# First raw pieces of the down product ahead of the last stores, the output weights split in the SSD's end, the mLSTM block's last iterations reordered

## The reference

```
x = x + (silu(h @ w_ffn_gate) * (h @ w_ffn_up)) @ w_ffn_down        # first block, last step
...
y_ssd = ssd_mixer(...)            # second block; scan over 8 chunks of 128 tokens
y_ml  = mlstm_mixer(...)          # the same chunks, 8 heads of 128
x  = x + concatenate([y_ssd, y_ml]) @ w_out
h2 = rmsnorm_2(x, norm2_w)
x  = x + hier_moe(h2, router_g_w, ..., exp_w_gate, exp_w_up, exp_w_down)
# hier_moe: best of 4 groups, then the best 2 of its 8 experts, for each token
```

## Time and the profile before

| quantity | value |
|---|---|
| median of 3 runs | 3291.56 us (3291.55 to 3295.12) |
| the profiled execution, its own time | 3288.88 us |
| its span in the profile | 3287.0 us |
| mean granted TensorE clock | 0.963 of full speed |
| PE busy | 3031.3 us, 92% of the span |
| PEld busy | 2485.2 us, 76% |
| DVE busy | 2204.8 us, 67% |
| ACT busy | 1617.9 us, 49% |
| POOL busy | 679.5 us, 21% |

### The profile page before, as it was taken

One profiled execution on the slowest core, in us unless ns is written; L12 is line 12 of the kernel. 1 busy time (PEld: TensorE's weight loads), 2 busy tenths in 40 slices (PEclk: granted clock), 3 DMA queues, 4 the chain that ended last, 5 costly groups with the idle time before them and its releaser, 6 DMA issues. The chain is left out here.

```text
span 3287.0 us, 38738 instructions
## 1 busy us (share of the span) xinstructions
PE 3031.3 (92%) x13814; PEld 2485.2 (76%) x13814; DVE 2204.8 (67%) x2760; ACT 1617.9 (49%) x2341; POOL 679.5 (21%) x553
## 2 busy tenths in 40 slices
PE   6999999899999999999899999979868779999994
PEld 4777777687878888788678886767767668888883
DVE  6668677624344545489477775449666579999997
ACT  6554444411343333345445443344354358888883
POOL 4222222100132222000322221134132111111100
PEclk9999999999999999999899999989989879999997
DMA  3222222442322223577254333352153079999995
GB/s 91 71 85 78 85 85 84 155 134 83 128 66 95 77 77 97 192 266 253 86 122 122 110 103 106 108 198 97 65 185 131 33 295 390 394 386 380 377 376 225
DMA packets 386898, 533.40 MB, mean 162 GB/s; under 512 B 68240, under 2 KB 268944, under 8 KB 385712
## 3 DMA queue, kind: packets, MB, share of 16 engines
q1 hardware_dynamic: 368064, 480.80, 42.4%
q0 software_dynamic: 18672, 50.49, 4.1%
HBM read 458.71 MB, written 89.26 MB: 167 GB/s over the span
## 5 line engine op out<-in xcount | busy, mean ns | idle before, releaser
L3883 DVE TENSOR_TENSOR h_hl<-ex_stage,h_hl 128x1024 fp32r<-128x1024 f32 x256 | 304.7, 1219 | 36.4 <-ACT h_hl L3879 34.7
L3879 ACT ACTIVATE h_hl<-ex_stage 128x1024 fp32r<-128x1024 f32 x256 | 271.2, 1061 | 74.3 <-PE ex_ps_d L430 24.3
L428 PE MATMUL m_ps<-m_t,m_ring 128*128 128x512 f32 x432 | 173.0, 400 | 13.4 <-DVE m_sga L842 5.0
L429 PE MATMUL m_ps<-m_t,m_ring 128*128 128x512 f32 x432 | 169.2, 392 | 0.0
L430 PE MATMUL m_ps<-m_t,m_ring 128*128 128x512 f32 x432 | 169.2, 392 | 0.0
L3883 DVE TENSOR_TENSOR ex_w_hl<-ex_stage,ex_w_hl 128x1024 fp32r<-128x1024 f32 x128 | 155.1, 1232 | 9.7 <-ACT ex_w_hl L3879 9.3
L687 ACT ACTIVATE m_ring<-m_sums 128x512 fp32r<-128x512 f32 x108 | 67.7, 628 | 166.7 <-POOL m_sums L663 115.6
L3879 ACT ACTIVATE ex_w_hl<-ex_stage 128x1024 fp32r<-128x1024 f32 x128 | 134.9, 1055 | 25.3 <-DMA ex_stage<-in_exp_w_gate_dram 12.6
L1603 DVE TENSOR_TENSOR ff_ring<-ff_stage,ff_ring 128x512 fp32r<-128x512 f32 x63 | 60.1, 953 | 110.1 <-ACT ff_ring L1517 109.4
L428 PE MATMUL ff_ps<-ff_t_high,ff_ring 128*128 128x512 f32 x336 | 130.8, 389 | 0.9 <-DVE ff_up_odd L1622 0.9
L430 PE MATMUL ff_ps<-ff_t_high,ff_ring 128*128 128x512 f32 x336 | 130.7, 389 | 0.0
(11 more groups left out here) (673 smaller groups left out, 9275.4 us busy)
## 6 DMA issues: line engine op xcount, KB each, us to landing
ex_stage<-in_exp_w_gate_dram SPq DMA_DIRECT2D x128, 512.0 KB, 5.4
ex_stage<-in_exp_w_up_dram SPq DMA_DIRECT2D x128, 512.0 KB, 5.4
ex_stage<-in_exp_w_down_dram SPq DMA_DIRECT2D x128, 512.0 KB, 5.4
m_stage<-in_w_in_dram SPq DMA_DIRECT2D x56, 512.0 KB, 4.7
ff_act_raw<-scratch_act SPq DMA_DIRECT2D x77, 256.0 KB, 3.4
ff_down_raw<-in_w_ffn_down_dram SPq DMA_DIRECT2D x77, 256.0 KB, 4.3
pc_stage<-in_w_in_dram SPq DMA_DIRECT2D x36, 512.0 KB, 5.1
ff_stage<-in_w_ffn_gate_dram SPq DMA_DIRECT2D x22, 512.0 KB, 3.7
```

What stands on the lines that cost most here:

```text
L428: nc.tensor.matmul(out, w_hl[0], x_hl[0], start=first, stop=False, skip_group_check=further)
L429: nc.tensor.matmul(out, w_hl[0], x_hl[1], start=False, stop=False, skip_group_check=further)
L3879: nc.scalar.activation(w_hl[u][:, 0], stage[:, s], ACT.Copy).then_inc(s_hi, 1)
L3883: nc.vector.tensor_tensor(w_hl[u][:, 1], stage[:, slot(e, u)], f32(w_hl[u][:, 0]), ALU.subtract).then_inc(s_lo, 1)
```

## The change

It has three parts. **In the feed-forward**, the raw buffers and slots are laid out anew, so that the third and fourth raw buffers are free when product 7 of the last block is done. SP issues the loads of steps 0 and 1 before the last store but one, those of steps 2 and 3 before the last store. `down_high(2)`, `down_low(1)` and `down_low(2)` move ahead of the last block's end. **In the SSD's end**, rows 0 to 6 of the mLSTM half of `w_out` are loaded in three DMAs (2, 2 and 3 rows of 128x1024) over the place of their low parts, and split there by seven ACT copies and seven DVE subtractions; in the mLSTM only the last row is left (two loads, two ACT copies, two POOL subtractions). `rows_g` is now requested ahead of queries and keys, and `chunk_loads(2)` and the gain row follow two weight loads instead of sixteen. **In the mLSTM's last iterations** the order on PE, DVE and ACT is written out; `choose` is cut into `group`, `best` and `second`, with additions and norms between them; the last chunk's split `y` has a buffer of its own, so that it waits for no output product; ACT's squares of tiles 6 and 7 use another scratch tile.

```diff
@@ hidden_memory
-    slot_at = [t_at(0, 0), t_at(1, 0), t_at(0, 1), t_at(0, 2), t_at(1, 2), t_at(0, 3), t_at(1, 3)]
+    slot_at = [t_at(0, 0), t_at(1, 0), t_at(0, 1), t_at(0, 3), t_at(1, 3), ring_at, ring_at + t_bytes]
...
-    raw_a = [room_at, t_at(1, 1), room_at + 2 * piece, ring_at]
-    raw_b = [room_at + piece, t_at(1, 1) + piece, ring_at + piece, ring_at + 2 * piece]
+    raw_a = [room_at, t_at(1, 1), room_at + 2 * piece, t_at(0, 2) + piece]
+    raw_b = [room_at + piece, t_at(1, 1) + piece, t_at(0, 2), t_at(1, 2)]
@@ feed_forward
-                product_done(eng, at[NF - 1, (5, 5, 6, 7, 7, 4, 4)[e]])
+                product_done(eng, at[NF - 1, (5, 5, 6, 4, 4, 3, 3)[e]])
...
                 elif e == 2:
-                    product_done(sp, N - 1)
+                    product_done(sp, at[NF - 1, 7])
...
-            for q in range(NF - 3, NF - 1):
-                store(q)
+            store(NF - 3)
             load(0)
             load(1)
+            store(NF - 2)
+            load(2)
+            load(3)
             store(NF - 1)
-            load(2)
-            for e in range(3, NE):
+            for e in range(4, NE):
...
+                elif seq[n - NR] == (NF - 1, 4):
+                    down_high(2)
             silu(NF - 1, 1, s_c12, NF - 1)
...
                     down_low(0)
+                    down_low(1)
                 elif seq[n - NR] == (NF - 1, 4):
-                    down_low(1)
+                    down_low(2)
             odd_act(NF - 1)
@@ ssd_chunks
+        FETCHED = (2, 4, NK)
+        w1_raw = Over(nc, at_hl + 8 * W * 4, at_hl + 16 * W * 4).take("w1_raw", [P, NK, W])
...
+            sp.wait_ge(p_state, NC)
+            sp.wait_ge(d_y, NC)
+            for sem, lo, hi in zip(s_w1, (0,) + FETCHED, FETCHED):
+                sp.dma_start(w1_raw[:, lo:hi], w1_v[:, lo:hi]).then_inc(sem, 16)
...
+            def w1_high(n):
+                act.wait_ge(s_w1[sum(n >= hi for hi in FETCHED)], 16)
+                nc.scalar.activation(hl[:, 0, n], w1_raw[:, n], ACT.Copy).then_inc(s_w1hi, 1)
...
+            def w1_low(n):
+                dve.wait_ge(s_w1hi, n + 1)
+                v.tensor_tensor(hl[:, 1, n], w1_raw[:, n], f32(hl[:, 0, n]), ALU.subtract)
...
+                if k == NC - 1:
+                    add(k - 1, (0,))
+                    w1_low(0)
+                    add(k - 1, (1,))
...
+            for n in range(1, NK):
+                w1_low(n)
             add(NC - 1)
@@ mlstm_chunks, SP
+                wait(sp, g_w, k - 2)
+                sp.dma_start(rows_g[:, b].rearrange("p h n -> p (h n)"), every(scr.rows[k, 0])).then_inc(s_rows[b], 16)
                 sp.dma_start(queries(k), scr.qk[k][:, 0:H]).then_inc(s_qk[b], 16)
                 sp.dma_start(keys(k), scr.qk[k][:, H:]).then_inc(s_qk[b], 16)
-                wait(sp, g_w, k - 2)
...
-            for n in range(NW):
-                h, k = divmod(n, KT)
-                low_ready(sp, n - NS)
-                sp.dma_start(stage[n % NS], w_v[:, k, h * HALF:(h + 1) * HALF]).then_inc(s_w[n % NS], 16)
-                if n == NW - 1:
-                    chunk_loads(2)
-                if n == NW - 1:
-                    sp.dma_start(gain_b[:], A.norm2_w_2[0].rearrange("(a n) -> a n", a=1).broadcast_to([P, W])).then_inc(s_gr, 16)
+            for h in range(2):
+                sp.dma_start(last_row_of[h], w_v[:, KT - 1, h * HALF:(h + 1) * HALF]).then_inc(s_w[h], 16)
+            chunk_loads(2)
+            sp.dma_start(gain_b[:], A.norm2_w_2[0].rearrange("(a n) -> a n", a=1).broadcast_to([P, W])).then_inc(s_gr, 16)
@@ mlstm_chunks, DVE, after the last chunk's query
+            gated(NC - 1)
+            y_low(NC - 1)
+            logits(NC - 4)
+            routing_tables()
+            group()
+            add(NC - 2, 1)
+            gained(NC - 3)
+            inverted(NC - 2)
+            normed_low(NC - 3)
+            best()
+            add(NC - 1, 0)
+            gained(NC - 2)
+            logits(NC - 3)
+            normed_low(NC - 2)
+            second()
+            early_totals()
+            add(NC - 1, 1)
+            logits(NC - 2)
+            inverted(NC - 1)
+            early_ranks()
+            gained(NC - 1)
...
+            early_slots(range(4))
+            normed_low(NC - 1)
+            early_slots(range(4, 2 * r.EARLY))
+            logits(NC - 1)
@@ mlstm_chunks, PE, last iteration and after it
+                if k == NC - 1:
+                    y_turn(k)
                 if 0 <= k - 3:
                     logit(k - 3)
...
+            out_product(NC - 1, 0)
+            normed_turn(NC - 2)
+            logit(NC - 3)
+            out_product(NC - 1, 1)
+            logit(NC - 2)
...
+            normed_turn(NC - 1)
+            logit(NC - 1)
```

More of the change, by code:

```diff
@@ L2609, in first_chunk, with ssd_chunks @@
     return head
-def ssd_chunks(nc, A, x_tm, at_hl, w2, scr, done, head, o_stored):
+def ssd_chunks(nc, A, x_tm, at_hl, w2, hl, scr, done, head, o_stored):
     NC, H, G, W = scr.T, SSD_HEADS, SSD_GROUPS, 1024
@@ L2774, in _ @@
                     decay(k + 1, 1)
+                else:
+                    for n in range(2):
+                        w1_high(n)
                 act.wait_ge(d_yt, 2 * k + 2)
@@ L2780, in _ @@
                 if k == NC - 1:
+                    for n in range(2, NK):
+                        w1_high(n)
                     act.wait_ge(head.g_w, 1)
@@ L3239, in _ @@
                 if k == 0:
-                    for n in range(6):
-                        w_high(n)
-                if t == 0:
-                    lows_ready(act, NW)
-                if t >= 0:
-                    act.wait_ge(d_add, 2 * t + 2)
-                    wait(act, n_lo, t)
-                    nc.scalar.activation(xg[:].rearrange("p k n -> p (k n)"), x_tm[:, t], ACT.Square,
-                                         accum_out=ssq[:, t:t + 1]).then_inc(n_sq, 1)
+                    w_high(0)
+                    w_high(1)
+                if 0 <= t < NC - 2:
+                    squares(t)
                 if k < NC:
@@ L3251, in _ @@
                     nc.scalar.activation(sm[:, STD], sm[:, VAR], ACT.Sqrt, scale=1.0 / D, bias=eps[:]).then_inc(a_std, 1)
-                if t >= 0:
-                    act.wait_ge(n_sq, t + 1)
-                    nc.scalar.activation(std[:, t:t + 1], ssq[:, t:t + 1], ACT.Sqrt, scale=1.0 / W, bias=eps[:]).then_inc(n_std, 1)
+                if 0 <= t < NC - 2:
+                    deviation(t)
                 if k < NC:
@@ L3269, in _ @@
                     nc.scalar.activation(r_hl[:, :, 0], r_st[:], ACT.Copy).then_inc(s_rhi, 1)
[L3270 to L3283 removed]
+                if 0 <= t < NC - 1:
+                    if t < NC - 2:
+                        scaled(t)
+                    if k == NC - 1:
+                        y_high(k)
+                        squares(t + 1)
+                        deviation(t + 1)
+                    normed_high(t)
+                    if k == NC - 1:
+                        scaled(t + 1)
+                if k < NC - 1:
+                    y_high(k)
+            squares(NC - 1)
+            deviation(NC - 1)
+            scaled(NC - 1)
+            normed_high(NC - 1)
         @block.vector
@@ L3569, in _, with normed_turn, y_turn @@
             pe.wait_ge(d_cs, 1)
-            for k in range(NC + 3):
-                if k < NC:
-                    numerators(k)
-                    updates(k, 0)
-                    updates(k, 1)
+            def normed_turn(t):
+                pe.wait_ge(n_xn, t + 1)
+                turn("x", t, lambda h: xn[:, h * P:(h + 1) * P])
+            def y_turn(k):
+                pe.wait_ge(a_hn, NJ * (k + 1))
+                turn("y", k, lambda h: h_r[:, h])
+            for k in range(NC):
+                numerators(k)
+                updates(k, 0)
+                updates(k, 1)
@@ L3600, in route @@
+            mm(ps_rank, r.before[:], r.early_o, start=True, stop=False)
+            mm(ps_rank, r.ones[:], r.early_counts[:, 0:r.EARLY], start=False, stop=True).then_inc(r_ranked, 1)
+            normed_turn(NC - 1)
+            logit(NC - 1)
 def route(nc, A, hl, scr, c, block, mem, r):
@@ L4332, in program @@
             done = [s for s in USED if s is not o_stored[0] and not any(s is k for k in head.sems)]
-            ssd_chunks(nc, A, x_tm, at_hl, w2_hl, scr, done, head, o_stored)
+            ssd_chunks(nc, A, x_tm, at_hl, w2_hl, hl, scr, done, head, o_stored)
             done = [s for s in USED if not any(s is k for k in head.sems)]
```

266 lines of the change are left out of this document (128 added, 138 removed).

## The result

| | before | with the change |
|---|---|---|
| median | 3291.56 us (4 runs) | 3264.89 us (3263.34 to 3268.53, 4 runs) |
| ratio to before | 1 | 0.9926, 95% interval 0.9913 to 0.9938 |
| profiled execution, own time | 3288.88 us | 3268.53 us |
| its span | 3287.0 us | 3266.7 us |

The change makes the kernel 26.7 us faster by the medians, 24.4 by the ratio. The number on record was 3261.5 (-30), so the direction and the size hold. The profiled execution is the slowest of its four, and stages that the change doesn't touch differ by some 2 us between two traces. So stages are compared here by their own lengths, from an event at their start to one at their end.

What follows compares the result with a forecast made beforehand. PE, busy for 92% of the span, bounds the kernel, so gains come only where it stands still: -5 + 0 - 13 - 12 = -30 from 3288.88, 3258.9; 3261.5 us for the median, range 3255 to 3275.

Steps and rivals of the forecast that it cites:

- Feed-forward, -5 forecast: Down product: earlier loads of steps 2 and 3 remove PE's 4.42 us wait; -5 us, bounds -3 and -6.
- what counts is how far that stream moves: Down product: loads and splits set its end; 1.05 MB leaving the place behind the store shifts them 3.4 us.
- SSD's end, 0 forecast: SSD's end: added loads, copies and subtractions hide in ACT's and DVE's idle time; 0, bounds 0 and +7 us.
- The rival of a late first piece: SSD's end: DMAs share engines evenly, last chunk's addition and gating wait 7 us; 3268.5 us, chance 0.07.
- its dating row: SSD's end: ACT's row at 2345.12 dates the last chunk's y and first load; piece expected 4.4 us later.
- Head, -13 forecast: mLSTM's head: earlier rows_g and gain row, fewer splits bring DVE's state update forward; -13 us, bounds -6 and -14.
- Tail, -12 forecast: mLSTM's tail: no wait for y's split, choice cut in pieces, block ends earlier; -12 us, bounds -6 and -14.
- one such collision costs 1.9 us: Tail: one small DVE instruction of the choice is blocked by POOL's rows_out, costing 1.9 us.
- the rival of POOL hitting the interleaved choice: Tail: all three rows_out hit two-input DVE instructions, 5.7 us; tail gives -8, 3265.5 us; chance 0.10.
- the second half takes the 7.1 us of before or less: Tail: chunk 7's second half takes 7.1 us or less, so is added at 2609 to 2611 instead of 2619.05.
- the 14 that the sum had for that case: Tail: large bound of the gain, -14 us, before a collision is counted against it.
- Slower by late keys: mLSTM iterations: rows_g's request ahead delays keys for front in six iterations; +9 at 6.5 us each, 3300; chance 0.02.

Runs made afterwards that it cites:

- e2: Kernel before with the feed-forward's part, the SSD's end split and the head's requests, but the old tail: 3272.81 us, ratio 0.9942.
- e1: Kernel before with the feed-forward's part of the change alone: 3286.89 us, ratio 0.9994.
- e4: Changed kernel with rows_out of tile 6 held back behind the gain multiplication and one two-input placing instruction moved behind tile 7's: 3259.02 us, ratio 0.9903.
- e5: e4 plus, from chunk 2 on, POOL's scaling of the state held back until DVE has written y's low part: 3251.7 us, ratio 0.9882.
- e8: Changed kernel with rows_g requested behind queries and keys again: 3268.56 us, ratio 0.9934.
- e3: Kernel before with only the order of SP's requests in the mLSTM's head changed, all sixteen half rows still there: 3289.98 us, ratio 0.9997.
- e6: e1 with the activations' low part written for 64 of 512 columns only from the down product's eighth step: 3278.23 us, ratio 0.9967.
- e7: Kernel before with the activations' low part written for 64 of 512 columns only from the down product's eighth step: 3284.46 us, ratio 0.9984.

## Why the prediction was right, point by point

The sum was right in sign and near in size (-30 forecast, -24 to -27 measured), because the three places where PE stood still were the right ones and what the head saves is not lost behind it (e2: steady iterations 133.11 and tail 67.72 us, against 132.83 and 67.76). The head came out as forecast. The other two terms were mis-sized, both toward too much.

- **Feed-forward, -5 forecast: -2 to -4 measured.** By e1's medians it is 2.1 us. By the traces the product is 224.11 to 228.76 us long in the six that have the part and DVE's full work (e1, e2, the changed kernel, e4, e5, e8), 226.6 on average, and 228.95 and 231.61 in the two without (before, e3): 3.6 us. The changed kernel's own 228.76 is the longest of the six, so the 0.2 us of the table above is no measure of the part. The step that was mis-sized is "what counts is how far that stream moves", with two steps' transfer time as its shift. The first window showed DVE busy for half of it, and later ones were not asked: in 1450 to 1480 and 1510 to 1540 DVE is busy for over 29 of 30 us. There part of the earlier start is given back in waits for DVE, and e6 and e7 show that with a lighter DVE it is not. The other part went with the clock, which the sum left out at this end: in e1, the changed kernel, e5 and e8 it takes 12.4 us from the last wait's end to the last matmul, in e2 and e4 10.8 as in the kernel before.
- **SSD's end, 0 forecast: 0 measured.** The stretch from chunk 6's to chunk 7's addition is 11.65 us long in e2 against 11.69 before. The changed kernel's own 12.92 has no new wait in it: PE waits 3.45 us for the split of `y` there, as before and in e2; its granted clock over 2350 to 2370 is 0.83 and e2's 0.91. The rival of a late first piece fell: it was there 5.1 us behind its dating row.
- **Head, -13 forecast: -11 by the changed kernel's trace, -14 by e2's (chunk 2's numerators).** The path was as described, from `rows_g` to the gain row to the state's update, which comes 10.97 us earlier in the one and 12.83 in the other. What the text passed over is that the request order brings nothing without the removed loads (e3). `rows_g` ahead makes the mask 3.3 us earlier (e8); in the time that is not clear of the spread.
- **Tail, -12 forecast: -7.1 by the trace, -7.9 by the medians, -5.3 by the ratios.** The reordered pieces did what was said: no wait for the split of `y`, additions between the pieces. Two costs in the sum were too small. One is the price of the collisions, "one such collision costs 1.9 us". There were two on the path, 4.15 us together (e4), and the first cost more than its own length, as PE stood still behind it and went on at a lower clock. This is the rival of POOL hitting the interleaved choice, which gave -8. The other is "the second half takes the 7.1 us of before or less". Those 7.09 us are DVE's wait ahead of an addition that itself came late, and the new order puts the turned rows of tile 6 and the logits of tile 5 on PE between the two halves. The two additions lie 12.1 us apart in the changed kernel and 10.5 in e4, where they were 8.2 before. So without the collisions the tail gains 11.2 us (56.53 us long), not the 14 that the sum had for that case.
- **Slower by late keys: fell.** The steady iterations lost 2 us over five, but e2 and e4, with the same order of requests, 0.3 and 0.7 (133.11 and 133.54 against 132.83), and in none of the three does PE wait for a DMA there.

The Trainium skill (SBUF — State Buffer, Who interferes with whom) states the rule for these pairs: a two-input DVE instruction from SBUF and a GpSimd instruction that reads SBUF don't run side by side, whoever comes second waits. Here 2.19, 2.61 and 2.69 us against 0.33, 0.48 and 1.23 agree with it, and the moved instructions of e4 and e5 confirm it. What the pairs cost in time was found from the rows, and in the iteration of 28.27 us the clock was the greater part of it.

What stays open is when the clock falls behind the last wait of the down product. It did behind 2.27, 2.48, 3.06 and 2.27 us (the changed kernel, e1, e5, e8), and did not behind 2.29, 2.39, 2.10 and 1.99 (before, e2, e3, e4). So neither the change nor the length of this wait decides it alone.

## What to carry to other kernels

Ahead of costing a removed wait, read the busy share of the engine that will pace the stage next, in windows as short as the stage, not over the whole: a nearly full engine gives part of an early start back. Before one request is moved up in an in-order queue, see what then waits behind it: here six loads did, and the move alone was worth nothing. Where DVE reads two operands from SBUF beside a POOL instruction, look for durations above their like and move POOL's start behind DVE's instruction by a wait: two such waits and one moved instruction, without any work removed, were worth some 13 us here by the medians, half as much as the whole change.

## What the runs showed of the hardware that was not expected

A blocked instruction of 1.46 us on DVE in a steady iteration made that iteration 2.56 us longer: PE's wait grew by only 0.96, and its granted clock over the iteration fell from 1.00 to 0.94. Other iterations with the same wait of 2.34 us kept 1.00 and took 26.65 to 26.68 us (the last steady ones of before, e2 and e4). In the tail PE's matmuls went from 0.30 to 0.41 us within a microsecond behind a wait of 2.25 us. Between chunk 7's two additions the granted clock was 0.74 there (2589.5 to 2602.6), and 0.84 in e4 (2583 to 2593.7), where that wait was 0.57.
